# A fused decoder kernel: early weight splits, two and a half units ahead of each pre-norm, and narrow RWKV products moved to the layer's beginning

## The reference

```python
for i in range(DEPTH):
    h = h + 0.5 * rms_norm(swiglu(rms_norm(h, ng[0]), w_in, w_out), ng[1])
    u = rms_norm(h, ng[2])
    out = gdn_mixer(u, ...) if i % 2 == 0 else rwkv_mixer(u, ...)
    h = h + rms_norm(out, ng[3])
    h = h + 0.5 * rms_norm(swiglu(rms_norm(h, ng[4]), w_in, w_out), ng[5])
```

```python
x_prev = concatenate([shift_prev[:, None], x[:, :-1]], axis=1)      # the token before
xs = x[:, :, None] + (x_prev - x)[:, :, None] * lerp                # six mixed inputs
r, k, v = xs[0] @ w_r, xs[1] @ w_k, xs[2] @ w_v                     # 1024 x 1024 each
xw, xa, xg = xs[3], xs[4], xs[5]
logw = -softplus(-(w0 + tanh(xw @ w1) @ w2)) - 0.5                  # w1: 1024 x 64
a = sigmoid(a0 + (xa @ a1) @ a2)                                    # a1: 1024 x 64
g = sigmoid(xg @ g1) @ g2                                           # g1: 1024 x 128
kk = l2_normalize(heads(k * k_k))                                   # 16 heads of 64
```

## Time and profile before

| what | value |
|---|---|
| median of 3 runs | 3194.11 us (3193.16 to 3195.04) |
| the profiled execution | 3197.23 us, of which the span of its instructions is 3195.4 us |
| TensorE busy, share of the span | 2789.5 us, 87% |
| VectorE, ScalarE, GpSimd busy | 39%, 27%, 34% |
| mean granted TensorE clock | 0.92 |

### The profile page before, as it was taken

The page is one execution under the profiler, slowest core; times in us unless marked ns, Lnnn a source line. Parts: engine busy times, 40 slices in busy tenths (PEclk is TensorE's granted clock), DMA queues, the critical chain, the costliest instruction groups (busy, mean ns, idle before and its releaser), DMA issues.

```text
span 3195.4 us, 60747 instructions
## 1 busy us (share of the span) xinstructions
PE 2789.5 (87%) x26393; PEld 2618.5 (82%) x26393; DVE 1242.2 (39%) x1468; ACT 866.6 (27%) x1185; POOL 1078.7 (34%) x514
## 2 busy tenths in 40 slices
PE   7999989787887899998999986875588677899997
PEld 6999989767865899998999976873488544899997
DVE  2333158715534433313333223335745325433312
ACT  3222232222212322223222222234133102422221
POOL 3444323314412244432444422322734011344432
PEclk9999989998978999999999998877699768999998
DMA  3223212210021222221222211210000001122221
GB/s 130 86 85 97 81 63 79 68 42 2 2 86 59 67 85 85 100 91 53 86 85 93 91 61 54 66 34 30 2 4 4 25 27 33 61 90 86 95 91 46
DMA packets 59724, 201.86 MB, mean 63 GB/s; under 512 B 14512, under 2 KB 14640, under 8 KB 59312
## 3 DMA queue, kind: packets, MB, share of 16 engines
q1 hardware_dynamic: 59568, 199.51, 18.8%
HBM read 189.81 MB, written 9.67 MB: 62 GB/s over the span
## 4 chain that ended last, share of the span: by engine, by line
PE 42%; issue 33%; POOL 11%; DVE 11%; ACT 1%; DMA 1%; DVEq 0%; POOLq 0%; SPq 0%; ACTq 0%
POOL wlo L258 10%; PE ps L288 9%; PE ps L286 9%; PE ps L287 9%; DVE cb L802 3%; PE ps L2032 1%; PE ps L2416 1%; PE ps L2040 1%; PE ps L553 1%; PE ps L2442 1%; DVE sFM L2211 1%; PE ps L1983 1%; PE ps L2443 1%; PE ps L1988 1%; PE ps L558 1%
## 5 line engine op out<-in xcount | busy, mean ns | idle before, releaser
L258 POOL TENSOR_TENSOR wlo<-raw,whi 128x1024 fp32r<-128x1024 f32 (+1 forms) x316 | 835.3, 2645 | 1516.2 <-ACT whi L250 1516.2
L286 PE MATMUL ps<-xh,whi 128*128 128x272 f32 x3776 | 1106.4, 293 | 61.5 <-POOL wlo L258 40.6
L288 PE MATMUL ps<-xh,wlo 128*128 128x272 f32 x3776 | 1104.6, 293 | 0.0
L287 PE MATMUL ps<-xl,whi 128*128 128x272 f32 x3776 | 1097.8, 291 | 0.0
L286 PEld LDWEIGHTS ps<-xh,whi 128*128 128x128 f32 x3776 | 722.2, 191 | 77.2 <-POOL wlo L258 38.9
L287 PEld LDWEIGHTS ps<-xl,whi 128*128 128x128 f32 x3776 | 724.1, 192 | 0.0
L288 PEld LDWEIGHTS ps<-xh,wlo 128*128 128x128 f32 x3776 | 721.7, 191 | 0.0
L250 ACT ACTIVATE whi<-raw 128x1024 fp32r<-128x1024 f32 (+1 forms) x316 | 354.4, 1124 | 1275.1 <-PE ps L288 1228.3
L288 PE MATMUL ps<-mh,wlo 128*128 128x272 f32 x1408 | 406.1, 288 | 0.0
L287 PE MATMUL ps<-ml,whi 128*128 128x272 f32 x1408 | 405.4, 288 | 0.0
L286 PE MATMUL ps<-mh,whi 128*128 128x272 f32 x1408 | 405.0, 288 | 0.0
(11 more groups left out here) (440 smaller groups left out, 3094.5 us busy)
## 6 DMA issues: line engine op xcount, KB each, us to landing
raw<-w SPq DMA_DIRECT2D x252, 512.0 KB, 3.5
raw<-w SPq DMA_DIRECT2D x64, 704.0 KB, 4.0
h<-xT SPq DMA_DIRECT2D x1, 2176.0 KB, 11.4
yT<-h SPq DMA_DIRECT2D x1, 2176.0 KB, 6.6
Sst<-state_gdn SPq DMA_DIRECT2D x4, 512.0 KB, 3.6
SG<-state_gdn SPq DMA_DIRECT2D x4, 512.0 KB, 3.6
gdn_s_s<-gG SPq DMA_DIRECT2D x4, 512.0 KB, 2.7
gdn_s_s<-gT SPq DMA_DIRECT2D x4, 512.0 KB, 2.6
```

The costliest lines, as they stand in the source:

```text
L258: pool.tensor_tensor(wlo[two][:, 0:kt * P], raw[slot][:, 0:kt * P], whi[two][:, 0:kt * P].bitcast(F32), ALU.subtract).then_inc(w_lo, 1)
L286: pe.matmul(o, wh, hi[:, r, :], start=(start and k == 0), stop=False)
L287: pe.matmul(o, wh, lo[:, r, :], start=False, stop=False)
L288: mm = pe.matmul(o, wl, hi[:, r, :], start=False, stop=(stop and k == kt - 1))
```

## The change

Six things change.

1. **Early splits.** While the last unit of a product is multiplied, ScalarE and GpSimd already split the first units of the next one (`early_hi`, `early_lo`); units 0 and 1 get buffers of their own (`EARLY`), units 2 and 3 use `whi` and `wlo`. This holds for the four FFN inputs, `gdn_in` and the new first product of the RWKV layer. ScalarE also takes the square root of one constant there (`warm`).
2. **Two and a half units abreast.** In these products units 0, 1 and the first half of unit 2 are multiplied tile by tile, then unit 2's second half, and only then the norm is spread and unit 3 multiplied. The sums of squares and the spread rows move to unused columns of the PSUM banks.
3. **Order in `post_norm_dve`.** The low part of tile m-1 is written between the two operations of tile m instead of behind them.
4. **Narrow products first.** The RWKV layer begins with `lora`, now four units on the plain (unshifted, unscaled) input: W and lerp times W, for `w1` with `a1` and for `g1`. By linearity x W + (x_prev - x)(lerp W) is the old result, so the shift by one token and the norm are applied to the products (`lora_dve`) and not to the inputs. The lerp is multiplied into the raw weights by VectorE (`lora_scale_dve`). The carried state of the sample group enters through 48 matmuls of 8 columns (`carried`). Three of the six mixed inputs go.
5. **Shift in halves.** r's mixed input is made from four tiles first; the second four are normalised and shifted between tiles 3 and 4.
6. **Key norms in v's time.** Squares and sums of the keys run beside v's units, and the root comes ahead of the sigmoids.

```diff
-    ("r", NM, NM), ("k", NM, NM), ("v", NM, NM), ("lora", 3, NM), ("wo", NM, NM),
+    ("lora", 4, NM), ("r", NM, NM), ("k", NM, NM), ("v", NM, NM), ("wo", NM, NM),
...
+        def early_hi(act, name, j):
+            n = BASE[name] + j
+            act.wait_ge(raw_in[n % 4], 16 * (n // 4 + 1))
+            if name == "lora" and j > 1:
+                act.wait_ge(R["lw_up"], past(R["lw_up"], j - 1))
+            free = 2 * (BASE[name] - (j < 3))
+            if free > 0:
+                act.wait_ge(acc, free)
+            dst = EARLY[name][0][j] if j < 2 else whi[n % 2]
+            act.activation(dst[:, 0:NM * P], raw[n % 4][:, 0:NM * P], ACT.Copy).then_inc(w_hi, 1)
+        def early_lo(pool, name, j):
+            n = BASE[name] + j
+            pool.wait_ge(w_hi, n + 1)
+            hi, lo = (EARLY[name][0][j], EARLY[name][1][j]) if j < 2 else (whi[n % 2], wlo[n % 2])
+            pool.tensor_tensor(lo[:, 0:NM * P], raw[n % 4][:, 0:NM * P], hi[:, 0:NM * P].bitcast(F32), ALU.subtract).then_inc(w_lo, 1)
...
+        def behind_norm_mm(pe, name, q):
+            behind_norm_tiles(pe, name, q)
+            behind_norm_half(pe, name)
+            spread_norm_pe(pe, q)
+            unit_mm(pe, name, 0, 3, pair(3), xh, xl)
+        def behind_norm_tiles(pe, name, q):
+            base = BASE[name]
+            bufs = [(EARLY[name][0][j], EARLY[name][1][j]) for j in range(2)] + [(whi[base % 2], wlo[base % 2])]
+            for k in range(NM):
+                pe.wait_ge(x_lo, 8 * SETS[name] + k + 1)
+                for j in range(3):
+                    if k == 0:
+                        pe.wait_ge(w_lo, base + j + 1)
+                    if j == 1:
+                        square_sum_pe(pe, q, k)
+                    first_products(pe, j, k, *bufs[j], halves=(0, 1) if j < 2 else (0,))
+            if q:
+                pe.wait_ge(h_upd, 8 * (q // 2))
+        def behind_norm_half(pe, name):
+            two = BASE[name] % 2
+            for k in range(NM):
+                first_products(pe, 2, k, whi[two], wlo[two], halves=(1,))
...
-                dve.tensor_tensor(tb[3][:, :, :], y[:, 2 * m:2 * m + 2, :], pair(3), ALU.mult).then_inc(h_tmp, 1)
+                dve.tensor_tensor(tb[3][:, :, :], y[:, 2 * m:2 * m + 2, :], post_rows(), ALU.mult).then_inc(h_tmp, 1)
+                if sett is not None and m:
+                    pre_norm_low(dve, q + 1, sett, m - 1)
                 dve.wait_ge(h_tmp, base + m + 1)
                 dve.scalar_tensor_tensor(h[:, 2 * m:2 * m + 2, :], tb[3][:, :, :], step,
                                          h[:, 2 * m:2 * m + 2, :], ALU.mult, ALU.add).then_inc(h_upd, 1)
-                if sett is not None and m:
-                    pre_norm_low(dve, q + 1, sett, m - 1)
...
-        def third_fourth_mm(pe, name, q):
-            spread_norm_pe(pe, q)
-            unit_mm(pe, name, 0, 2, pair(2), xh, xl)
-            pe.wait_ge(rs_full, q // 2 + 1)
-            unit_mm(pe, name, 0, 3, pair(3), xh, xl)
...
+                    if last and j == 3:
+                        act.activation(warm[:, q // 2:q // 2 + 1], eps[:, 0:1], ACT.Sqrt)
+                        if then == "ffn3_in":
+                            act.wait_ge(R["so0"], past(R["so0"], 64))
+                            act.wait_ge(R["so1"], past(R["so1"], 64))
+                        if then is not None:
+                            for jj in range(2 if then == "lora" else 3):
+                                early_hi(act, then, jj)
...
+                if i == 0 and m % 4 == 0:
+                    shift_dve(dve, m // 4)
...
+        def rkv_pair(i, m):
+            return pair(m % (3 if i == 2 else 4))
...
+                    if i == 2:
+                        key_square_act(act, u + j)
+        def key_square_act(act, m):
+            if m == 0:
+                act.wait_ge(x_lo, 8 * SETS["wo"])
+            if m - 1 > 0:
+                act.wait_ge(R["kq_mm"], past(R["kq_mm"], m - 1))
+            act.activation(tb[m % 2][:, :, :], wh(k_, m), ACT.Square, scale=v(V_KK + m)).then_inc(R["kq_sq"], 1)
+        def key_sum_pe(pe, m):
+            pe.wait_ge(R["kq_sq"], past(R["kq_sq"], m + 1))
+            sum_rows(pe, pair(3), two_cols[:, 14 - 2 * m:30 - 2 * m], tb[m % 2], m == 0, m == NM - 1).then_inc(R["kq_mm"], 1)
...
+                if i == 2 and m > 2:
+                    key_sum_pe(pe, m - 3)
+            if i == 2:
+                for m in range(NM - 3, NM):
+                    key_sum_pe(pe, m)
...
+        def lora_scale_dve(dve):
+            for j, parts in ((2, ((3, slice(0, 64)), (4, slice(64, P)))), (3, ((5, slice(0, P)),))):
+                n = BASE["lora"] + j
+                dve.wait_ge(raw_in[n % 4], 16 * (n // 4 + 1))
+                w = raw[n % 4][:, 0:NM * P].rearrange("p (m c) -> p m c", c=P)
+                for i, c in parts:
+                    lerp = vec[:, V_LERP + i * NM:V_LERP + (i + 1) * NM].unsqueeze(2).broadcast_to([P, NM, c.stop - c.start])
+                    mul = dve.tensor_tensor(w[:, :, c], w[:, :, c], lerp, ALU.mult)
+                mul.then_inc(R["lw_up"], 1)
+            dve.wait_ge(R["sh_hi"], past(R["sh_hi"], 1))
+            dve.tensor_tensor(sh_l[:, :, :], shin[:, :, :], sh_h[:, :, :].bitcast(F32), ALU.subtract).then_inc(R["sh_lo"], 1)
+        def shift_dve(dve, part):
+            lo, n = 4 * part, 4
+            for m in range(lo, lo + n):
...
         def lora_act(act):
+            base = BASE["lora"]
+            early_hi(act, "lora", 2)
+            early_hi(act, "lora", 3)
+            act.wait_ge(R["sh_in"], past(R["sh_in"], 16))
+            act.activation(sh_h[:, :, :], shin[:, :, :], ACT.Copy).then_inc(R["sh_hi"], 1)
+            pre_norm_act(act, 8, SETS["lora"])
...
+        def lora_out_act(act):
+            act.wait_ge(R["lora_up"], past(R["lora_up"], 12))
+            act.activation(lt1[0:64, :, :], LT[0][0:64, :, :], ACT.Tanh)
+            act.activation(lt1[64:P, :, :], LT[0][64:P, :, :], ACT.Copy).then_inc(R["lora_cp"], 1)
+            act.activation(lg[:, :, :], LT[1][:, :, :], ACT.Sigmoid).then_inc(R["lora_cp"], 1)
+            act.wait_ge(R["lora_cp"], past(R["lora_cp"], 2))
...
+            def carried(j):
+                n = base + j
+                pe.wait_ge(w_lo, n + 1)
+                o = ps[:, 6, HALF + NB * (j - 2):HALF + NB * (j - 1)]
+                for k in range(NM):
+                    wh_, wl_ = (t[n % 2][:, k * P:(k + 1) * P] for t in (whi, wlo))
+                    pe.matmul(o, wh_, sh_h[:, k, :], start=(k == 0), stop=False)
+                    pe.matmul(o, wh_, sh_l[:, k, :], start=False, stop=False)
+                    pe.matmul(o, wl_, sh_h[:, k, :], start=False, stop=(k == NM - 1))
+            behind_norm_tiles(pe, "lora", 8)
+            pe.wait_ge(R["sh_lo"], past(R["sh_lo"], 1))
+            carried(2)
+            behind_norm_half(pe, "lora")
+            carried(3)
+            pe.wait_ge(R["lora_raw"], past(R["lora_raw"], 2))
+            spread_norm_pe(pe, 8)
+            unit_mm(pe, "lora", 0, 3, pair(3), xh, xl)
...
+            up = R["lora_up"]
+            dve.wait_ge(R["lora_raw"], past(R["lora_raw"], 4))
+            for g in range(2):
+                here, prev = LT[g], LT[2 + g]
+                n = past(up, 6 * g)
+                dve.tensor_tensor(prev[:, :, :], prev[:, :, :], rs[:, :, :], ALU.mult).then_inc(up, 1)
+                dve.tensor_tensor(here[:, :, :], here[:, :, :], rs[:, :, :], ALU.mult).then_inc(up, 1)
+                dve.wait_ge(up, n + 2)
+                dve.tensor_tensor(here[:, :, :], here[:, :, :], prev[:, :, :], ALU.subtract).then_inc(up, 1)
...
-            pe.wait_ge(R["lora_cp"], past(R["lora_cp"], 3))
+            pe.wait_ge(R["lora_cp"], past(R["lora_cp"], 2))
+            pe.wait_ge(R["r_cp"], past(R["r_cp"], 24))
+            pe.wait_ge(R["kq_rt"], past(R["kq_rt"], 1))
...
-            pre_norm_act(act, 8, None)
+            lora_act(act)
             for i, (name, dst) in enumerate((("r", r_), ("k", k_), ("v", v_))):
+                rkv_act(act, i, name, dst)
                 if i == 0:
-                    act.wait_ge(R["sh_out"], past(R["sh_out"], 16))
-                rkv_act(act, i, name, dst)
-            lora_act(act)
+                    lora_out_act(act)
             prep_act(act)
...
-            shift_dve(dve)
-            for i in range(6):
-                mix_dve(dve, i)
+            norm_dve(dve, 8)
+            mix_dve(dve, 0)
+            shift_out_dve(dve)
+            lora_dve(dve)
+            mix_dve(dve, 1)
+            mix_dve(dve, 2)
...
-            post_norm_dve(dve, 7, 0.5)
+            lora_scale_dve(dve)
+            post_norm_dve(dve, 7, 0.5, SETS["lora"])
```

235 lines of the change are left out of this document (127 added, 108 removed).

## The result

The median fell from 3194.57 to 3138.45 us (four runs of each on one chip): the ratio is 0.9825, with a 95% interval of 0.9808 to 0.9842, 56 us. On a second chip, with five runs against nine, it was 0.9816 (0.9801 to 0.9831). The prediction said 3131.6 with 3116 to 3149 as range. So the direction was right, the time fell inside the range, and the forecast was some 7 us too low. The profiled execution took 3138.25 us with a span of 3136.5.

A forecast was written before the change was run, and what follows sets the result against it. TensorE, busy 87%, was taken to bound the kernel, with losses where it stands: behind pre-norms, at RWKV's beginning and after v. Starts -21.5 and RWKV -41.0 make -62.5 us: median 3131.6 us, range 3116 to 3149.

The forecast's parts named there:

- gdn_in: the step that failed: Start of gdn_in behind its pre-norm: first wait 4.8 instead of 3.8, so 5.5 us less.
- FFN starts: Starts behind pre-norms: 4.5 us less each for ffn1_in, ffn2_in, ffn3_in, 1.2 for ffn0_in; root's table wait three times 0.45.
- Late weights: Rival: early weight splits come late, third unit waits 1.9 again; starts gain 10 instead of 21.5, 3143 us; chance 0.10.
- Post-norm ahead of RWKV: Post-norm before the RWKV layer: VectorE's `sh_l` ahead of the reciprocal makes the spread post-norm 3.2 us later.
- Narrow products: RWKV's beginning: from spread post-norm to the narrow products' end 40.3 us, with 48 products of 8 columns at 0.1 each.
- Shift in halves: r's mixing in the RWKV layer: r's first two units end at 1972.7, 18.4 us late, TensorE waiting for tile 3.
- Between r and k: Two table loads and three activations ahead of k's splits: 4.4 us more, k's first product 11.3 behind r's end.
- Key norms: Four sums between v's units cost 3.8 us; v's end to the key norms' spreading 16.7 against 84.3, 67.6 less.
- The slower one: Rival: the 48 carried 8-column products make the kernel slower; at 2.0 us each 3223 us; chance 0.03.
- The one of nothing gained: Rival: the 84.3 us behind v is work that comes back, r, k, v 67 late instead of 26.6; 3194 us; chance 0.02.
- the starts' 21.5: Sum of all gains at starts behind norms, FFN inputs and gdn_in together: 21.5 us, with 10 to 28 as bounds.

The follow-up runs named there:

- again: The changed kernel run and profiled a second time, unchanged, against the kernel before on the same chip: ratio 0.9816.

## Why the prediction was right, and where not

- **gdn_in: the step that failed.** "In gdn_in the first wait is 4.8 instead of 3.8, which makes 5.5" measured as a loss of 0.1. The 5.5 was taken from TensorE's waits, in a stage in which VectorE sets the end. For VectorE two things happened, and neither was in the sum: its chain starts 29.8 from S instead of 25.8, since the third group of products in each tile and the half unit now stand ahead of the norm, and it is 3.95 shorter. The two cancel. This term is 5.6 of the miss. The profiles' spans differ by 58.9 where 62.5 was forecast; `ffn2`, RWKV and the rest of the DeltaNet layer lack 1.9 more, and `ffn0`, `ffn1`, `ffn3` and the recurrence gave 3.8 beyond the forecast, so the total is nearer than this part by luck. The other 3 of the 7 us are no step of the working: the profiled execution before lay 2.7 above its median, the one after 0.2 below.
- **FFN starts: right, slightly small.** 5.7 (4.9 again) and 5.8 for 4.5 plus 0.45 in `ffn1` and `ffn3`, and 3.2 for 1.7 in `ffn0`; the four units of `ffn1_in` end 34.6 from S (1096.06 less 1061.43; 35.8 again), for 35.5. Early weights are the larger part (3.3 to 4.2 in `ffn1`), the half unit 0.9 to 1.5 (`ffn2`, `ffn3`). Late weights, the rival, did not happen in the changed kernel.
- **Post-norm ahead of RWKV: right.** The sums' end to S takes 3.8 longer; 3.2 was forecast, and the reciprocal stands behind `sh_l` as written. The run that moves `sh_l` won it back at S, and lost most of it in the next stretch.
- **Narrow products: right.** 40.3 forecast; 43.1 in the first profile and 40.9 in the second. A product of 8 columns starts every 0.112, not 0.1. The Trainium skill, TensorE: Matmul & The Clock Gate, section LDWEIGHTS, gives 107 ns for loading 128 columns by its formula, an estimate, which is near that row.
- **Shift in halves: right.** r's first pair ends 66.9 from S (65.4 again), forecast 66.0, with TensorE's wait in the middle. GpSimd's two low parts at 1933.2 and 1939.3 made two rows of VectorE 2.1 and 2.0 longer than the same rows without them, for 2.4 each in the forecast.
- **Between r and k: right,** 11.65 for 11.3, and shown by the run that moves the activations.
- **Key norms: right, but for the sums between v's units.** 16.6 from v's last product to the beginning of the spreading for 16.7 (the terms given for it add up to 16.5); the four sums between v's units cost 4.8 instead of 3.8. TensorE waits once in v, 3.0 ahead of the third unit, as it did before. The table load and root are in the rows of ScalarE as forecast:

```profile
2138.22 1.28 ACT L1994 ACT_TABLE_LOAD   x1
2139.51 0.70 ACT L1994 ACTIVATE tb<-ps,eps 16x544 f32<-16x544 f32 x1
2140.24 1.28 ACT L1998 ACT_TABLE_LOAD   x1
2141.55 0.71 ACT L1998 ACTIVATE RA<-ps,vec 128x544 f32<-128x544 f32 x1
```

- **The rivals.** The slower one needed 1.3 us above 0.1 for each carried product; the row shows 0.112. The one of nothing gained is put at 3194, but with r, k and v 67 late its own terms leave the starts' 21.5, which makes 3172; r's first pair came at most 0.9 later than forecast.

What stays open: whether the copy of the norm ahead of unit 4's split would turn the earlier spread in `gdn_in` into time (by its rows VectorE could start near 24.5 from S instead of 29.8, with one low part of GpSimd more in its chain); this was not tried.
